# Slot tables in two transfers an expert ahead, spare rows turned later, the first expert's rows whole: one layer of a mixture-of-experts decoder

## The reference, cut to what matters

```python
# x: (1, 1024, 1024) float32; one layer
proj = x @ w_in;  mix = concat(conv, attention, gated linear attention) @ w_out
x = layer_norm(ALPHA * x + mix)
# grouped_moe: 16 experts in 4 groups, the best group, its best 2 experts
scores = sigmoid(t @ router_w)
gate = ...                       # (1024, 16), two nonzero per token
for e in range(16):
    h = silu(t @ w1[e]) * (t @ w3[e])        # 1024 -> 512
    y = y + gate[:, e:e+1] * (h @ w2[e])     # 512 -> 1024
x = layer_norm(ALPHA * x + y)
```

## Time and profile before

| | |
|---|---|
| median of 3 runs | 976.55 us (976.47 to 983.02) |
| the profiled execution: its time | 981.02 us |
| its span, first to last instruction | 979.3 us |
| mean granted TensorE clock | 0.973 |
| PE / DVE / ACT / POOL busy, share of span | 93% / 64% / 49% / 29% |
| expert blocks | from about 558 us to 940 us of the span |

### The profile page before, as it was taken

One profiled execution on the slowest core, in us unless ns is written; L12 is line 12 of the kernel. 1 busy time (PEld: TensorE's weight loads), 2 busy tenths in 40 slices (PEclk: granted clock), 3 DMA queues, 4 the chain that ended last, 5 costly groups with the idle time before them and its releaser, 6 DMA issues.

```text
span 979.3 us, 17611 instructions
## 1 busy us (share of the span) xinstructions
PE 913.9 (93%) x6611; PEld 707.4 (72%) x6611; DVE 631.5 (64%) x831; ACT 482.2 (49%) x755; POOL 284.0 (29%) x292
## 2 busy tenths in 40 slices
PE   8999999999999999979999898999999999998970
PEld 6778998996777777768887475776777767775750
DVE  4211833665564755676556886878787878777885
ACT  3212532225564654561224424666666666665683
POOL 3000000000000000050000486666666666666443
PEclk9999999999999999999999799999999999999995
DMA  9301121001100031059432289999999989999973
GB/s 259 69 22 44 44 58 30 1 2 44 44 22 23 25 73 44 1 182 394 143 129 86 82 245 270 310 334 337 310 324 318 325 299 329 336 330 274 333 261 145
DMA packets 103438, 168.90 MB, mean 172 GB/s; under 512 B 26300, under 2 KB 49980, under 8 KB 103376
## 3 DMA queue, kind: packets, MB, share of 16 engines
q1 hardware_dynamic: 88720, 143.74, 43.2%
q0 software_dynamic: 11616, 23.14, 9.6%
q10 hardware_dynamic: 3040, 1.19, 0.5%
HBM read 143.81 MB, written 24.54 MB: 172 GB/s over the span
## 4 chain that ended last, share of the span: by engine, by line
PE 56%; POOL 16%; DMA 10%; issue 8%; DVE 6%; ACT 3%; POOLq 0%; SPq 0%; DVEq 0%; ACTq 0%
PE bank L887 11%; PE bank L889 11%; PE bank L888 11%; DMA tab<-slot_tokens 9%; PE pz L1003 3%; PE bank L1081 2%; POOL xg L759 2%; POOL tabQ L746 2%; PE pz L887 2%; PE pz L889 2%; PE pz L888 2%; PE bank L1097 2%; POOL sum_scratch L774 2%; POOL sum_scratch L779 2%; POOL slot_tokens L685 2%
## 5 line engine op out<-in xcount | busy, mean ns | idle before, releaser
L1975 DVE TENSOR_TENSOR el<-er,eh 128x1024 fp32r<-128x1024 f32 x192 | 223.6, 1218 | 18.2 <-ACT eh L1568 18.2
L1568 ACT ACTIVATE eh<-er 128x1024 fp32r<-128x1024 f32 x192 | 189.8, 1050 | 7.7 <-PE pz L889 7.7
L632 POOL MEMSET rw<- 128x128 f32 x1 | 0.2, 206 | 415.5 <-DVE mix L1899 415.5
L1906 DVE TENSOR_TENSOR_SCAN Qs<-Qs,own 128x128 f32<-128x128 f32 (+7 forms) x48 | 65.0, 1355 | 69.7 <-ACT Qs L1455 69.7
L887 PE MATMUL pz<-eh,xh 128*128 128x512 f32 x256 | 104.4, 408 | 4.4 <-DVE el L1975 4.4
L887 PE MATMUL bank<-xT_hi,w_hi 128*128 128x512 f32 (+1 forms) x264 | 106.1, 402 | 1.9 <-DVE xT_lo L1791 1.9
L889 PE MATMUL bank<-xT_hi,w_lo 128*128 128x512 f32 (+1 forms) x264 | 102.4, 388 | 0.0
L888 PE MATMUL bank<-xT_lo,w_hi 128*128 128x512 f32 (+1 forms) x264 | 101.8, 386 | 0.0
L888 PE MATMUL pz<-el,xh 128*128 128x512 f32 x256 | 100.8, 394 | 0.0
L889 PE MATMUL pz<-eh,xl 128*128 128x512 f32 x256 | 100.8, 394 | 0.0
L887 PE MATMUL bank<-w_hi,xT_hi 128*128 128x384 f32 x192 | 65.0, 338 | 1.3 <-ACT kteN L1470 1.3
(11 more groups left out here) (337 smaller groups left out, 1873.7 us busy)
## 6 DMA issues: line engine op xcount, KB each, us to landing
er<-in_w_dram SPq DMA_DIRECT2D x192, 512.0 KB, 7.3
w_raw<-in_w_in_dram SPq DMA_DIRECT2D x21, 512.0 KB, 3.9
x_row<-in_x_dram SPq DMA_DIRECT2D x8, 512.0 KB, 9.0
xres<-in_x_dram SPq DMA_DIRECT2D x8, 512.0 KB, 5.6
sum_scratch<-x SPq DMA_DIRECT2D x8, 512.0 KB, 3.9
x_scratch<-x1p SPq DMA_DIRECT2D x8, 512.0 KB, 2.6
cx<-sum_scratch SPq DMA_DIRECT2D x8, 512.0 KB, 8.1
out_dram<-cx SPq DMA_DIRECT2D x5, 512.0 KB, 3.0
```

The lines of the kernel that those rows point to most:

```text
L1568: act.activation(eh[:, p, :], er[:, p, :], ACT.Copy).then_inc(S["eh_ok"], 1)
L1906: dve.tensor_tensor_scan(Qs[:, h, 0:W][:, ::-1], Qs[:, h, 0:W][:, ::-1], own1[:, T - W:][:, ::-1], 0.0, ALU.mult, ALU.max).then_inc(S["sca ...
L1975: dve.tensor_tensor(el[:, p, :], er[:, p, :], eh[:, p, :].bitcast(F32), ALU.subtract).then_inc(S["el_ok"], 1)
```

## The change

- The slot table of an expert comes in two transfers instead of five, and slots are dealt over the blocks in another order so that each descriptor of the second is 40 bytes. It is asked for one expert ahead.
- `step(r, b)` on POOL becomes: `quarters` of b, `gather` of b, `load_table` of b+1, `gates` of b-2, `add_rows` of b-2.
- `spare_turn` of b+1 on DVE moves from behind `hB` to behind `hTl`; `rows_turn` keeps its place.
- Expert 0: its 128 rows are gathered whole in one indirect transfer from `sum_dram` (4 KB each), TensorE transposes them into PSUM (`first_transposes`), ACT and DVE split them from there in two halves. Two `spin(4)` go.
- The direct slots of experts 1 and 2 are made by one product of 128 slots, a mask and a selection product (`slot_masks`, `spread_slots`, `quarter_rows`) instead of four products by quarter.
- The second 8 scatters stand behind `first_gather(2)`.

The diff, cut: the rest of it declares tiles, adjusts counts of semaphores, repeats the POOL order for the blocks ahead of the loop, and calls the new functions below in the order named above.

```diff
                 pool.indirect_dma_start(xg[b % 2][:, NB - 1, :], None, x1_quarters, bass.IndirectOffsetOnAxis(firstQ[:, b, NB - 1:NB], 0))\
                     .then_inc(S["xgB_in"], 16)
                 pool.wait_ge(S["first_ok"], 2 * b + 2)
-                for c in range(NB - 1):
+                if b == 0:
+                    pool.indirect_dma_start(xgAs[0][:, :], None, sum_dram, bass.IndirectOffsetOnAxis(firstA[:, 0:1], 0)).then_inc(S["xg_in"], 16)
+                for c in range(NB - 1) if b else ():
                     pool.indirect_dma_start(xg[b % 2][:, c, :], None, x1_quarters, bass.IndirectOffsetOnAxis(firstQ[:, b, c:c + 1], 0))\
                         .then_inc(S["xg_in"], 16)
 
             first_gather(0)
             pool.wait_ge(S["xgB_in"], 16)
-            pool.wait_ge(S["xg_in"], 16 * (NB - 1))
+            pool.wait_ge(S["xg_in"], 16)
             first_gather(1)
             scatter(0)
-            scatter(1)
             pool.wait_ge(S["xBt_ok"], 1)
             pool.wait_ge(S["xTt_ok"], 1)
             pool.wait_ge(S["xgB_in"], 32)
-            pool.wait_ge(S["xg_in"], 32 * (NB - 1))
+            pool.wait_ge(S["xg_in"], 16 * NB)
             first_gather(2)
+            scatter(1)
...
                 if not (isinstance(b, int) and b < 4):
                     pool.wait_ge(S["y_out"], 32 * (b - 3))
                     pool.sem_inc(S["pool_go"], 1)
-                pool.dma_start(tab[r][:, 0:2], idl_dram[bass.ds(b * TW, P), :]).then_inc(S["idx_in"], 16)
-                for g in range(NQ):
-                    pool.dma_start(tab[r][g * TR:(g + 1) * TR, 2:].rearrange("s (c o) -> s c o", c=NB),
-                                   idl_dram[bass.ds(b * TW, TW), :].rearrange("(c s) o -> s c o", c=NB)).then_inc(S["idx_in"], 16)
+                rows = idl_dram[bass.ds(b * TW, TW), :].rearrange("(s c) o -> c s o", c=NB)
+                blocks = idl_dram[bass.ds(b * TW, TW), :].rearrange("(s c) o -> s (c o)", c=NB)
+                pool.dma_start(tab[r][:, 0:2], rows[0:NQ]).then_inc(S["idx_in"], 16)
+                pool.dma_start(tab[r][:, 2:], blocks.unsqueeze(0).to_broadcast([NQ, TR, 2 * NB])).then_inc(S["idx_in"], 16)
...
-            def step(r, b):
-                load_table(r, b)
-                gates((r + 2) % 4, b - 2)
+            def step(r, b, ahead=True):
                 quarters(r, b)
                 gather(r, b)
+                if ahead:
+                    load_table((r + 1) % 4, b + 1)
+                gates((r + 2) % 4, b - 2)
                 add_rows((r + 2) % 4, b - 2)
 
...
+                    load_table(0, b0 + 4)
+                with pool.Fori(2 if isinstance(j, int) else 1, NE // 4 - 1) as i:
                     for u in range(4):
                         step(u, b0 + 4 * i + u)
+                for u in range(4):
+                    step(u, b0 + NE - 4 + u, u < 3)
...
             def slot_tokens(b):
 
-                for part, blocks in enumerate(((NB - 1,), range(NB - 1))):
-                    pe.wait_ge(S["oneh_ok"], 2 * b + part + 1)
-                    for c in blocks:
-                        for i in range(NT):
-                            for g in range(NQ):
-                                last = pe.matmul(sids_bank[b % 2][1 - part][g * TR:(g + 1) * TR, 2 * c:2 * c + 2],
-                                                 oneh[:, b % 2, i, c * TR:(c + 1) * TR], idb[:, :, i],
-                                                 start=(i == 0), stop=(i == NT - 1), skip_group_check=True)
-                    last.then_inc(S["sids_ps"], 1)
+                n = 3 * b - 1 if b else 0
+                pe.wait_ge(S["oneh_ok"], n + 1)
+                for i in range(NT):
+                    for g in range(NQ):
+                        last = pe.matmul(sids_bank[b % 2][1][g * TR:(g + 1) * TR, 0:2], oneh[:, b % 2, i, P:TW], idb[:, :, i],
+                                         start=(i == 0), stop=(i == NT - 1), skip_group_check=True)
+                last.then_inc(S["sids_ps"], 1)
+                pe.wait_ge(S["oneh_ok"], n + 2)
+                for i in range(NT):
+                    last = pe.matmul(sids_bank[b % 2][0][:, 0:2], oneh[:, b % 2, i, 0:P], idb[:, :, i], start=(i == 0), stop=(i == NT - 1),
+                                     skip_group_check=True)
+                last.then_inc(S["sids_ps"], 1)
+
+            def spread_slots(b):
+
+                pe.wait_ge(S["oneh_ok"], 3 * b + 2)
+                pe.matmul(sids_bank[b % 2][0][:, 2:2 + 2 * NQ], selm[:, :], spm[:, b, :, :].rearrange("p g o -> p (g o)"), start=True, stop=True,
+                          skip_group_check=True).then_inc(S["sids_ps"], 1)
 
             def slot_gates(b):
...
             slot_tokens(0)
             spin(6)
             slot_gates(0)
-            spin(4, po[:, 0:GLA_W])
             slot_tokens(1)
             slot_gates(1)
-            spin(4, po[:, 0:GLA_W])
-
-            def spare_gu(b):
-
-                pe.wait_ge(S["xBt_ok"], b + 1)
-                for q in range(NF):
+
+            def first_transposes():
+
+                pe.wait_ge(S["xg_in"], 16)
+                for k in range(NK):
+                    last = pe.transpose(xb[k // 4][:, k % 4, :], xgAs[0][:, k * P:(k + 1) * P], ident[:, :])
+                last.then_inc(S["xTt_ok"], 1)
+
+            def spare_gu(b, qs=range(NF)):
+
+                if qs[0] == 0:
+                    pe.wait_ge(S["xBt_ok"], b + 1)
+                for q in qs:
                     for p in (q, NF + q):
                         pe.wait_ge(S[f"e_in{p}"], 16 * b + 16)
...
             def pe_block(b, nxt, buf=0, nbuf=0):
-                spare_gu(b)
-                pe.wait_ge(S["xTl_ok"], b + 1)
+                if first_block(b):
+                    spare_gu(b, range(0, 2))
+                    pe.wait_ge(S["selm_ok"], 3 * NQ + 2)
+                    spread_slots(1)
+                    first_transposes()
+                    spare_gu(b, range(2, NF))
+                else:
+                    spare_gu(b)
+                pe.wait_ge(S["xTl_ok"], b + 2)
                 rows_gu(b, 0)
                 if first_block(b):
                     slot_tokens(2)
@@ -1293,6 +1324,8 @@
                 pe.wait_ge(S["hB_ok"], b + 1)
                 pe.transpose(pz[1][:, 2 * P:3 * P], hB[:, :], ident[:, :]).then_inc(S["hTB_ps"], 1)
                 rows_gu(b, 1)
+                if first_block(b):
+                    spread_slots(2)
...
                 act.wait_ge(S["xTt_ok"], b + 1)
-                act.activation(xh[:, :, :], xT[:, :, :], ACT.Copy).then_inc(S["xTh_ok"], 1)
+                if first_block(b):
+                    for r in range(2):
+                        act.activation(xh[:, 4 * r:4 * r + 4, :], xb[r], ACT.Copy).then_inc(S["xTh_ok"], 1)
+                else:
+                    act.activation(xh[:, :, :], xT[:, :, :], ACT.Copy).then_inc(S["xTh_ok"], 1)
...
-                dve.wait_ge(S["xg_in"], 16 * (NB - 1) * b + 16 * (NB - 1))
-                if not first_block(b):
-                    dve.wait_ge(S["piece_done"], (NPIECE - 1) * (b - 1) + 2 * NF)
+                dve.wait_ge(S["xg_in"], 16 * (NB - 1) * b + 16)
+                dve.wait_ge(S["piece_done"], (NPIECE - 1) * (b - 1) + 2 * NF)
...
-                dve.tensor_tensor(xl[:, :, :], xT[:, :, :], xh[:, :, :].bitcast(F32), ALU.subtract).then_inc(S["xTl_ok"], 1)
+                if first_block(b):
+                    for r in range(2):
+                        dve.wait_ge(S["xTh_ok"], r + 1)
+                        dve.tensor_tensor(xl[:, 4 * r:4 * r + 4, :], xb[r], xh[:, 4 * r:4 * r + 4, :].bitcast(F32), ALU.subtract)\
+                            .then_inc(S["xTl_ok"], 1)
+                else:
+                    dve.wait_ge(S["xTh_ok"], b + 2)
+                    dve.tensor_tensor(xl[:, :, :], xT[:, :, :], xh[:, :, :].bitcast(F32), ALU.subtract).then_inc(S["xTl_ok"], 1)
 
...
-            def slot_rows(b, part):
-
-                cs, bank = ((slice(NB - 1, NB), sids_bank[b % 2][1][:, 2 * NB - 2:2 * NB]),
-                            (slice(0, NB - 1), sids_bank[b % 2][0][:, 0:2 * NB - 2]))[part]
-                dve.wait_ge(S["sids_ps"], 2 * b + part + 1)
-                link(dve.tensor_scalar(sids[:, b, cs], bank[:, 0::2], quad[:, 0:1], None, ALU.add))
-                dve.tensor_tensor(firstQ[:, b, cs], bank[:, 1::2], sids[:, b, cs], ALU.add).then_inc(S["first_ok"], 1)
+            def spare_rows(b):
+
+                bank = sids_bank[b % 2][1]
+                dve.wait_ge(S["sids_ps"], 3 * b if b else 1)
+                link(dve.tensor_scalar(sids[:, b, NB - 1:NB], bank[:, 0:1], quad[:, 0:1], None, ALU.add))
+                dve.tensor_tensor(firstQ[:, b, NB - 1:NB], bank[:, 1:2], sids[:, b, NB - 1:NB], ALU.add).then_inc(S["first_ok"], 1)
+
+            def whole_rows():
+
+                bank = sids_bank[0][0]
+                dve.wait_ge(S["sids_ps"], 2)
```

(53 more changed lines are left out.)

7 lines of the change are left out of this document (3 added, 4 removed).

## The result

| | kernel before | changed kernel |
|---|---|---|
| median | 976.51 us (973.48 to 983.02, 4 runs) | 1004.73 us (1002.86 to 1006.04, 4 runs) |
| profiled execution: time / span | 981.02 / 979.3 us | 1003.6 / 1002.0 us |
| mean granted TensorE clock | 0.973 | 0.979 |

The ratio is 1.0278, with a 95% interval of 1.0223 to 1.0334: the change makes the kernel 28 us slower. I had predicted 1013, with a range of 998 to 1030.

A forecast was written before the change was run, and what follows sets the result against it. It took GpSimd's chain of table, gather and adds, a little longer than TensorE's block, to set the pace. 11 x 28.0 - 261.8 = +46.2, front -9.7, together +36.5 on 976.55: 1013 us, range 998 to 1030.

The forecast's parts named there:

- Rival 1: Blocks 3 to 14: gates come in time, 11 blocks at 23.09 us plus the gain in blocks 0 and 1; 959 us, chance 0.06.
- the front: Blocks 0 and 1: 3.9 us less in block 0 and 5.8 in block 1, together 9.7 us, bounds 5 to 12.
- buffer free and picked up: From a block's start of hA (H): spare turn ends at 3.3 us, GpSimd takes it up 0.6 later, H + 3.9.
- five gather issues: GpSimd's issues of one gather, before the table issues: 7.1 us, bounds 6.6 to 7.5.
- gates copied, after H: GpSimd's copy of the gates is done 13.0 us after the block's start of hA, where before it was 1.9.
- from there to the next hA: VectorE's work from piece 1's low part: eleven low parts, yA and hB, 13.5 us.
- likeliest case: Blocks 3 to 14: yB waits for gates behind the gather, period 28.0 us (27.2 to 28.8); 1001 to 1026 us, chance 0.84.
- The rule weighed: Shared VectorE and GpSimd port: gather issues in VectorE's idle time go fastest, 6.6 us, period 27.5, time 1008 us.
- Rival 2: Blocks 3 to 14: gates copied by H + 10 (H: start of hA), period 25.0 us; 980 us, no change, chance 0.04.
- what the moved scatters delay: Adds of block 0, table and gather of block 3: issues end near 615 us, rows turned near 621, no loss counted.
- The end: The stretch behind block 14 stays as it is, no change in time.
- Rival 3: TensorE's clock falls after its waits in each block, 11 x 1.2 to 11 x 2.4 us more; 1026 to 1039 us, chance 0.06.

The follow-up runs named there:

- e1: Changed kernel with the copy of the gates moved to the head of GpSimd's step, ahead of the gather; 974.64 us on chip A, 966.75 us on chip C.
- e2: Kernel before with only the copy of the gates of b-2 moved behind the gather of b; 1015.97 us on chip A, one run.
- e4: e1 with the adds of block 0 asked for behind the table of block 3; 963.67 us on chip B, 964.96 us on chip C.
- e7: e1 with all 16 scatters ahead of the gather of block 2 again; 967.14 us on chip B, one run.
- e9: Kernel before with only VectorE's spare turn moved from behind hB to behind hTl; 1005.47 us on chip C, ratio 1.0317.
- e3: Changed kernel with the spare turn put back behind hB for all blocks but the first; 999.64 us on chip A, one run.
- e8: e4 with the adds of block 1 ahead of the two table issues of block 4; 963.95 us on chip C, ratio 0.9883.

## Why the prediction was right

**The bound and the mechanism.** The wait that the change adds came as described: yB held 8.0 us by the copy of the gates, VectorE's low parts behind it, GpSimd waiting for the spare turn and no longer for tables. e1 takes it out and the period is 23.09; e2 puts it alone into the kernel before and the period is 25.61. Rival 1 (959) was refuted by the changed kernel. Without that order of the gates its period does come, e1's 23.09, but not its time (966.75 on chip C), as the front's gain went in block 2.

**The size: 28.0 was 26.7.** Counting from H, the terms and what they measured:

| term | predicted | measured |
|---|---|---|
| buffer free and picked up | 3.9 | 3.93 |
| five gather issues | 7.1 | 6.28 |
| two table issues | 1.2 | 1.45 |
| copy of the gates | 0.79 | 0.26 |
| gates copied, after H | 13.0 | 11.92 |
| yB to piece 1's low part | 1.4 | 1.46 |
| from there to the next hA | 13.5 | 13.35 |

So 1.3 us a block, of which 0.8 are the gather and 0.5 the copy. The 6.28 and the 26.72 lie below the bounds of my own likeliest case (6.6 to 7.5, and 27.2 to 28.8). Both terms I had taken from rows where VectorE was at work part of the time. In the new order they fall into its 8 us of idleness, and there the four later issues take 0.95 to 0.97 each where the earlier trace rows has a mean of 1.08. The rule weighed pointed the right way: by it the gather would take 6.6 us, and the trace has 6.28, lower even than that. But the copy or tensor_scalar that it speaks of isn't what stands beside the slow issues of the other traces; those are subtractions. The Trainium skill, page SBUF — State Buffer, section Who interferes with whom, also says that a VectorE instruction with two inputs in SBUF contends with a GpSimd instruction that reads SBUF, and infers that such a VectorE instruction doesn't hold up the writing of descriptors. The low parts are such instructions, and beside them issues took 1.88 to 1.94 us instead of 0.95 (e4), so the traces go with the first statement and not with the inference.

**The last interval.** I counted 11 at 28.0. The last has 25.23 because step 15 asks for no table behind its gather and its copy comes 1.45 earlier; read from the diff, it needed no trace. With the ten at 26.72, the intervals are 15.5 us under the sum. Rival 2 had the copy done at H + 10 and a period of 25.0; the measured 11.92 and 26.72 lie 1.9 and 1.7 above it, and 1.1 and 1.3 under mine.

**The front: -5.6 instead of -9.7.** Block 0 came 5.8 us earlier (574.29 against 580.10), where I had 3.9 and a bound of 6; from its transposes to those of block 1 it was the further 5.8 that I had, though not for my reason. I gave it to the scatters' new place, but e7 and e9 have the old place and take 23.1 us there too, both with the late spare turn. The late turn only moves the wait: in e9 block 2 then takes 28.4, as it takes 29.1 in the changed kernel, and from block 0 to block 3 the sum is 75.0 us before, 75.4 in e9 and 75.2 in the changed kernel. What the front kept is block 0. The step that failed is "what the moved scatters delay", put at nothing: I put the last gather issue near 615 and the turn near 621. It ended at 621.27, since 3.04 us for the scatters' landing and 7.37 for the table stood in it, and VectorE was ready at 620.25, with TensorE now 11.6 us earlier. So 6.0 us went back in block 2. e4 showed that this cover has two layers: with the table early, the adds are late next. The price of a gain at the front is read from what GpSimd has to finish by then, and that queue didn't get shorter by 11.6 us.

**The end** was 2.4 us shorter (60.0 against 62.4 us behind block 14). The rows place it behind the last issue of output rows, 970.85 before and 995.91 now: from there to the end of the span it is 8.45 us before, 8.2 and 8.4 in the two other traces with the old slot order (chips B and C), and 6.1 now, as in e1. Why those transfers end sooner stays open. Together: 36.5 - 15.5 + 4.1 - 2.4 = 22.7 us between the two profiled executions; between the medians it is 28.2, as the one of before lay 4.5 above its median and this one 1.1 below. So the 8.3 us between 1013 and the measured median are a sum of misses that don't all point one way: 15.5 and 2.4 too many, 4.1 and 5.5 too few. That a period outside my bounds still ended well inside the range is partly luck.

**Rival 3** (the clock falls) didn't come: with waits of TensorE of 1.4, 1.0 and 0.6 us a block the granted clock was 1.00 (2.4 GHz) over the stretch from 655 to 940 us, and the mean of the whole span 0.979, above the 0.973 of before.

## What to carry to other kernels

A small instruction moved behind a large one in an in-order queue inherits every wait of the large one: the 0.26 us copy that was put behind a gather cost 38.5 us in all, and nothing in its own cost says so. Before moving an instruction, write down who waits for it and what stands in front of it in the new place; if that is a buffer which the waiter itself has to free, the two engines take turns instead of overlapping. And when an engine's wait goes away, ask what runs undisturbed in it: here GpSimd's issues were fast (6.3 us a gather) while VectorE stood still, and took 9.1 where it didn't.

## What the hardware showed that I had not expected

**GpSimd's issues slow down beside VectorE's subtractions.** The same five gather issues take 6.28 us in the changed kernel, with VectorE idle, and 776.67 - 767.53 = 9.14 us in e4 (chip C). GpSimd's timeline of e4 there:

```profile
767.53 1.23 POOL L760 DMA_INDIRECT xg<-x_scratch,tabQ  x1 [5.58 <-DVE xB L2020]
769.07 1.88 POOL L763 DMA_INDIRECT xg<-x_scratch,tabQ  x1 [0.30 <-issue]
771.25 1.94 POOL L763 DMA_INDIRECT xg<-x_scratch,tabQ  x1 [0.30 <-issue]
773.50 1.91 POOL L763 DMA_INDIRECT xg<-x_scratch,tabQ  x1 [0.30 <-issue]
775.71 0.95 POOL L763 DMA_INDIRECT xg<-x_scratch,tabQ  x1 [0.30 <-issue]
```

and VectorE's of the same stretch, with a gap from 775.92 to 776.58, into which the one short issue falls:

```profile
767.75 4.62 DVE L2013 TENSOR_TENSOR el<-er,eh 128x1024 fp32r<-128x1024 f32 x4
...
773.36 2.36 DVE L2013 TENSOR_TENSOR el<-er,eh 128x1024 fp32r<-128x1024 f32 x2 [0.33 <-ACT eh L1602]
775.64 0.28 DVE L2305 TENSOR_TENSOR hB<-silB,pz 128x128 f32<-128x128 f32 x1
776.58 4.63 DVE L2013 TENSOR_TENSOR el<-er,eh 128x1024 fp32r<-128x1024 f32 x4 [0.65 <-ACT eh L1602]
```

Each VectorE subtraction takes 1.14 us, and the slow issues are up to 1.0 us longer, as if each stood through one. The gathers are steady: 6.1 to 6.3 us in every step of the changed kernel and of e3 from 652 us on, where VectorE stands, and 9.1 to 9.2 in those of e1 and e4 from 675 us on. Not every single issue is slow: in e9 an issue of 0.96 us started at 773.85, beside them. The copy of the gates took 0.26 us in idle time and 1.67 in e4, the table issues 0.78 and 1.36. That VectorE is the cause is read from these coincidences. The nearest test is e9, which moves one VectorE instruction and nothing else, and whose gather rises from 7.1 to 8.6 us in the mean; no run took the subtractions away.

**A table's latency doesn't follow its size or its number of transfers**: mostly 6 to 8 us from issue to use, five transfers or two. The lowest seen are 4.9 us in e8 (from 604.02 to 608.95) and 5.2 to 5.6 in e4 (5.6 from 604.78 to 610.42), all with no accumulating transfer just ahead of the table in GpSimd's queue; behind two of them it took 8.7 us in e8 (from 623.90 to 632.59) and 7.4 in the changed kernel.

**One chip was slower in one stretch only.** On chip A the products for the slot tokens and gates stood in pauses of 0.4 to 1.2 us that the page puts down to issue (at 568 to 574 in e1). They sum to 4.0 of the 8.2 us by which e1's block 0 is later than in the changed kernel's trace. Most of the rest is TensorE's clock: granted 0.51 from 561 to 564.5 us and 0.50 from 574 to 578 (1.2 GHz), where the changed kernel's trace has 1.00 (2.4 GHz) in the same products; the pauses stood before the second fall, and before the first a wait of 2.0 us that the changed kernel's trace has too. The kernel before took 24 us more there than on the other two. The cause of the pauses stays open.
